# Mixer stage of a two-layer decoder step: prompt division in the transposing product, convolution norm with tokens on partitions, negated scores without scaling, and the pooling product ahead of output parts

## The reference

```python
def conv_mixer(a, prev, dw, dw_bias, ln_g, ln_b, pw):
    g = a[..., :CONV_W] * jax.nn.sigmoid(a[..., CONV_W:])
    buf = jnp.concatenate([prev.astype(g.dtype), g], axis=1)
    y = lax.conv_general_dilated(buf, ...) + dw_bias
    y = jax.nn.silu(layernorm(y, ln_g, ln_b)) @ pw      # 256 channels
    return y, buf[:, -(CONV_K - 1):]

def sparse_attend(q, ks, vs, valid):                    # 8 heads of 64, 2 key-value heads
    s = jnp.einsum('btngd,btknd->btngk', qg, ks.astype(jnp.float32)) * HEAD_DIM ** -0.5
    s = jnp.where(valid[:, :, None, None, :], s, -jnp.inf)
    p = jax.nn.softmax(s, axis=-1)
    o = jnp.einsum('btngk,btknd->btngd', p, vs.astype(jnp.float32))
    return o.reshape(B, T, ATTN_W).astype(q.dtype)
```

## Time and profile before

| | |
|---|---|
| median of 3 runs | 1144.7 us (1140.73 to 1146.01) |
| the profiled execution's own time | 1138.1 us |
| its span, first to last instruction | 1136.4 us |
| mean granted TensorE clock | 0.988 |
| TensorE busy | 1078.3 us, 95% of the span |
| VectorE busy | 740.0 us, 65% |
| ScalarE busy | 513.5 us, 45% |
| GpSimd busy | 190.0 us, 17% |
| stretch of the change, layer 1 | about 296 to 340 us from the span's start |
| the same, layer 2 | about 854 to 900 us |

### The profile page before, as it was taken

The page is one execution under the profiler, slowest core; times in us unless marked ns, Lnnn a source line. Parts: engine busy times, 40 slices in busy tenths (PEclk is TensorE's granted clock), DMA queues, the critical chain, the costliest instruction groups (busy, mean ns, idle before and its releaser), DMA issues.

```text
span 1136.4 us, 27658 instructions
## 1 busy us (share of the span) xinstructions
PE 1078.3 (95%) x9374; PEld 1024.2 (90%) x9374; DVE 740.0 (65%) x1211; ACT 513.5 (45%) x830; POOL 190.0 (17%) x241
## 2 busy tenths in 40 slices
PE   6999999999779999999999999999987899999996
PEld 5999999988459999999999999998873799999995
DVE  5667744688975766764476666448889466777544
ACT  5544443631454644443464444345216455444432
POOL 4211100411311311110042111004212022111001
PEclk9999999999899999999999999999998999999998
DMA  8464565443536455555435465563345445555541
GB/s 282 163 229 150 220 210 195 162 142 107 152 97 203 134 183 183 185 185 178 155 112 193 176 232 179 198 245 122 114 139 143 100 154 190 179 181 184 185 148 39
DMA packets 90464, 191.17 MB, mean 168 GB/s; under 512 B 12322, under 2 KB 48482, under 8 KB 90402
## 3 DMA queue, kind: packets, MB, share of 16 engines
q1 hardware_dynamic: 87426, 184.82, 48.7%
q0 software_dynamic: 2976, 5.53, 2.1%
HBM read 187.71 MB, written 2.59 MB: 167 GB/s over the span
## 4 chain that ended last, share of the span: by engine, by line
PE 85%; DVE 6%; ACT 4%; issue 2%; SPq 1%; DMA 1%; POOL 0%; DVEq 0%; POOLq 0%; ACTq 0%
PE PS L1111 24%; PE PS L1112 23%; PE PS L1113 23%; PE PS L1219 4%; PE PS L1147 2%; PE PS L1249 2%; DVE w_lo L601 1%; SPq L264 1%; PE PS L1158 1%; PE PS L1159 1%; PE PS L1162 1%; DVE rstd_post L630 1%; ACT w_hi L380 1%; PE PS L1225 1%; PE PS L1481 1%
## 5 line engine op out<-in xcount | busy, mean ns | idle before, releaser
L601 DVE TENSOR_TENSOR w_lo<-raw,w_hi 128x1024 fp32r<-128x1024 f32 x295 | 394.6, 1338 | 307.9 <-ACT w_hi L380 305.4
L380 ACT ACTIVATE w_hi<-raw 128x1024 fp32r<-128x1024 f32 x295 | 310.7, 1055 | 250.7 <-PE PS L1113 209.9
L1111 PE MATMUL PS<-x_hi,w_hi 128*128 128x264 f32 x1456 | 415.7, 286 | 0.7 <-DVE w_lo L601 0.6
L1112 PE MATMUL PS<-x_lo,w_hi 128*128 128x264 f32 x1456 | 412.6, 283 | 0.0
L1113 PE MATMUL PS<-x_hi,w_lo 128*128 128x264 f32 x1456 | 412.3, 283 | 0.0
L1111 PEld LDWEIGHTS PS<-x_hi,w_hi 128*128 128x128 f32 x1456 | 274.2, 188 | 2.3 <-DVE w_lo L601 1.6
L1112 PEld LDWEIGHTS PS<-x_lo,w_hi 128*128 128x128 f32 x1456 | 274.4, 188 | 0.1
L1113 PEld LDWEIGHTS PS<-x_hi,w_lo 128*128 128x128 f32 x1456 | 273.0, 188 | 0.0
L1111 PE MATMUL PS<-h_hi,w_hi 128*128 (+1 forms) x832 | 237.2, 285 | 3.7 <-DVE h_lo L1054 3.7
L1113 PE MATMUL PS<-h_hi,w_lo 128*128 (+1 forms) x832 | 236.9, 285 | 0.0
L1112 PE MATMUL PS<-h_lo,w_hi 128*128 (+1 forms) x832 | 236.2, 284 | 0.0
(11 more groups left out here) (255 smaller groups left out, 994.8 us busy)
## 6 DMA issues: line engine op xcount, KB each, us to landing
raw<-in_wts SPq DMA_DIRECT2D x312, 512.0 KB, 3.7
kv<-in_kT SPq DMA_DIRECT2D x128, 64.0 KB, 2.0
kx<-in_kxT SPq DMA_DIRECT2D x128, 32.0 KB, 2.1
vx<-in_vC POOLq DMA_DIRECT2D x48, 64.0 KB, 2.3
raw<-in_vC SPq DMA_DIRECT2D x32, 64.0 KB, 2.3
kv<-in_vC SPq DMA_DIRECT2D x32, 64.0 KB, 2.0
out_yT<-h SPq DMA_DIRECT2D x8, 132.0 KB, 1.8
vx<-in_vC SPq DMA_DIRECT2D x16, 64.0 KB, 1.8
```

Of the source, the lines that this page charges most:

```text
L380: act.activation(w_hi[:, u % SPLIT, :], raw[:, u % RAW, :], ACT.Copy) \
L601: tt(w_lo[:, u % SPLIT, :], raw[:, u % RAW, :], w_hi[:, u % SPLIT, :].bitcast(F32), AL.subtract) \
L1111: pe.matmul(out, w_hi[:, w, cols], hi, start=start, stop=False)
L1112: pe.matmul(out, w_hi[:, w, cols], lo, start=False, stop=False)
```

## The change

- Prompt division. The probabilities stay undivided. VectorE makes four diagonal matrices from the identity and the four inverted sums (`share`, 128 x 4 x 128), and TensorE multiplies each 128x128 block of the exponentials by its diagonal, which transposes and divides at once, in place of the transpose. `share` has one buffer for all pairs, so VectorE waits for the previous pair's products before it writes it.
- Negated scores. Masking computes mask minus scores, the maximum becomes a minimum, and the exponential has scale -1 with the minimum as its bias. The scale moves into the multiplier with which the queries are rotated (`turned`). The small multiplications of the extremum by the scale are gone, for the prompt's pairs and for the sample group.
- Convolution norm. The variance sums are made with tokens on the partitions: products of the squares with a column of ones give up to 128 tokens on partitions in each of three columns. ScalarE takes the root of these columns, VectorE inverts them (`inverted`, after `norm(1)`), and TensorE spreads them over all partitions by a product with the identity, behind pair 1's transposing products. `normalized` then multiplies from PSUM.
- The pooling product and the two transposes of the sample group's output stand ahead of `out_part(1, (0, 1))` and `out_part(2, (0, 1))`, the pooling product first.

```diff
@@ ScalarE
-                            ins = act.activation(t, t, ACT.Exp, scale=SCALE,
+                            ins = act.activation(t, t, ACT.Exp, scale=-1.0,
...
-                        act.activation(crs[:, :], PS[:, 6, 0:NT], ACT.Sqrt, scale=1.0 / 256,
-                                       bias=epsb[:, 0:1]).then_inc(sem["c_rms"], 1)
+                        act.activation(crt[:, 0:2], PS[:, 6, 0:2], ACT.Sqrt, scale=1.0 / 256, bias=epsb[:, 0:1])
+                        act.activation(crt[0:NB, 2:3], PS[0:NB, 6, 2:3], ACT.Sqrt, scale=1.0 / 256,
+                                       bias=epsb[0:NB, 0:1]).then_inc(sem["c_rms"], 1)
...
-                act.activation(psm[:, :], psm[:, :], ACT.Exp, scale=SCALE,
-                               bias=smx[:, 1:2], accum_out=smx[:, 2:3]).then_inc(sem["p_sexp"], 1)
+                act.activation(psm[:, :], psm[:, :], ACT.Exp, scale=-1.0,
+                               bias=smx[:, 0:1], accum_out=smx[:, 2:3]).then_inc(sem["p_sexp"], 1)
@@ VectorE
-                turned(9, aq[:, 0, :])
+                turned(9, aq[:, 0, :], SCALE)
...
-                    linked(stt(s, bias[:, :].unsqueeze(1).to_broadcast([128, 2, 384]), -BIG, PS[:, 2:4, 0:384],
-                               AL.mult, AL.add))
-                    dve.tensor_reduce(spm[:, j % 2, 0:4:2], s[:, :, 0:256], AX.X, AL.max)
-                    k = step(L, dve.tensor_reduce(spm[:, j % 2, 1:4:2], s[:, :, 256:384], AX.X, AL.max))
-                    after(L, k)
-                    ts(spm[:, j % 2, :], spm[:, j % 2, :], -SCALE, None, AL.mult).then_inc(sem["s_masked"], 1)
+                    linked(stt(s, bias[:, :].unsqueeze(1).to_broadcast([128, 2, 384]), BIG, PS[:, 2:4, 0:384],
+                               AL.mult, AL.subtract))
+                    dve.tensor_reduce(spm[:, j % 2, 0:4:2], s[:, :, 0:256], AX.X, AL.min)
+                    dve.tensor_reduce(spm[:, j % 2, 1:4:2], s[:, :, 256:384], AX.X, AL.min) \
+                        .then_inc(sem["s_masked"], 1)
...
-                    for b, (lo, hi) in enumerate(((0, 256), (256, 384))):
-                        t = sp_[:, j % 2, :, lo:hi]
-                        ins = tt(t, t, sps[:, j % 2, b:4:2].unsqueeze(2).to_broadcast([128, 2, hi - lo]), AL.mult)
-                    ins.then_inc(sem["p_norm"], 1)
+                    if j:
+
+                        dve.wait_ge(sem["p_t"], at_layer(L, "p_t", 2 * j))
+                    tt(share[:, :, :], ident.unsqueeze(1).to_broadcast([128, 4, 128]),
+                       sps[:, j % 2, :].unsqueeze(2).to_broadcast([128, 4, 128]), AL.mult).then_inc(sem["p_norm"], 1)
...
+                def inverted():
+
+                    dve.wait_ge(sem["c_rms"], at_layer(L, "c_rms", 1))
+                    dve.reciprocal(crt[:, 0:2], crt[:, 0:2])
+                    dve.reciprocal(crt[0:NB, 2:3], crt[0:NB, 2:3]).then_inc(sem["c_inv"], 1)
+
                 def normalized():
 
-                    dve.wait_ge(sem["c_rms"], at_layer(L, "c_rms", 1))
-                    linked(dve.reciprocal(crs[:, :], crs[:, :]))
+                    dve.wait_ge(sem["c_wide"], at_layer(L, "c_wide", 1))
                     for c in range(2):
-                        ins = tt(cacc[:, c, :], cacc[:, c, :], crs[:, :], AL.mult)
+                        ins = tt(cacc[:, c, :], cacc[:, c, :], PS[:, 6, 0:NT], AL.mult)
...
                 norm(1)
+                inverted()
                 masked(2)
...
-                linked(dve.reduce_max(smx[:, 0:1], psm[:, :], AX.X))
-                ts(smx[:, 1:2], smx[:, 0:1], -SCALE, None, AL.mult).then_inc(sem["s_smax"], 1)
+                dve.tensor_reduce(smx[:, 0:1], psm[:, :], AX.X, AL.min).then_inc(sem["s_smax"], 1)
@@ TensorE
-                            ins = pe.transpose(PS[:, (7, 0)[a], 128 * n:128 * n + 128], p[:, c:c + 128], ident)
+                            ins = pe.matmul(PS[:, (7, 0)[a], 128 * n:128 * n + 128], p[:, c:c + 128],
+                                            share[:, 2 * a + c // 256, :], start=True, stop=True)
...
                         pe.wait_ge(sem["c_sq"], at_layer(L, "c_sq", 1))
-                        channel_sum(csq, "c_var")
+                        for b, n in enumerate((128, 128, NB)):
+                            for c in range(2):
+                                ins = pe.matmul(PS[0:n, 6, b:b + 1], csq[:, c, 128 * b:128 * b + n], ones[:, 0:1],
+                                                start=(c == 0), stop=(c == 1))
+                        ins.then_inc(sem["c_var"], 1)
+                    if j == 1:
+                        pe.wait_ge(sem["c_inv"], at_layer(L, "c_inv", 1))
+                        for b, n in enumerate((128, 128, NB)):
+                            ins = pe.matmul(PS[:, 6, 128 * b:128 * b + n], crt[0:n, b:b + 1].to_broadcast([n, 128]),
+                                            ident[0:n, 0:n], start=True, stop=True)
+                        ins.then_inc(sem["c_wide"], 1)
...
                 values(1)
-                out_part(1, (0, 1))
-                out_part(2, (0, 1))
+                pe.wait_ge(sem["pool_y"], at_layer(L, "pool_y", 1))
+                for c in range(2):
+                    ins = pe.matmul(PS[:, 4 + c, 0:NT], raw[:, w, col(4 + c)], pw[:, c, :], start=True, stop=True)
+                ins.then_inc(sem["unit_done"], 1)
                 pe.wait_ge(sem["o_sc"], at_layer(L, "o_sc", 1))
                 for c in range(2):
                     ins = pe.transpose(PS[:, 7, 128 * c:128 * c + 128], osb[:, c, :], ident)
                 ins.then_inc(sem["o_st"], 1)
-                pe.wait_ge(sem["pool_y"], at_layer(L, "pool_y", 1))
-                for c in range(2):
-                    ins = pe.matmul(PS[:, 4 + c, 0:NT], raw[:, w, col(4 + c)], pw[:, c, :], start=True, stop=True)
-                ins.then_inc(sem["unit_done"], 1)
+                out_part(1, (0, 1))
+                out_part(2, (0, 1))
```

More of the change, by code:

```diff
@@ L88 @@
     o_shi=1, o_slo=1, dg=1,
-    tanh=2, glu=2, stack=1, diag=2, conv=1, c_part=4, c_fold=1, conv_p=1, c_sum=1, c_cent=1, c_sq=1, c_var=1, c_rms=1, c_norm=1, c_silu=1,
+    tanh=2, glu=2, stack=1, diag=2, conv=1, c_part=4, c_fold=1, conv_p=1, c_sum=1, c_cent=1, c_sq=1, c_var=1, c_rms=1, c_inv=1, c_wide=1, c_norm=1, c_silu=1,
     conv_r=1, c_out=1, c_ohi=1, c_olo=1,
@@ L168, in build @@
         X = place("X", [128, NS], F32, s1)
-        crs = place("crs", [128, NT], F32, s1)
         assert s1[0] <= s1_end
         ties = place("ties", [128, NS], F32, [s2[0]])
+        share = place("share", [128, 4, 128], F32, [s2[0] + 4128])
         relu = place("relu", [128, 4, 256], F32, s2)
@@ L214, in build @@
         spread = place("spread", [128, 128], F32)
+        crt = place("crt", [128, 4], F32)
         assert s_kx[0] <= kx_end and s_gs[0] <= gs_end and s_sq[0] <= s_gs0
@@ L721, in rope, with turned @@
                     tt(x, x, tmp, AL.add).then_inc(sem["rope"], 1)
-                def turned(m, x):
+                def turned(m, x, scale=1.0):
                     turns[0] += 1
                     src = PS[:, m % 2, 0:NT]
-                    chunk(m, (x, src, (1.0, turn[:, 0, :])), (rtmp[:, turns[0] % 2, :], src, (1.0, turn[:, 1, :])))
+                    chunk(m, (x, src, (scale, turn[:, 0, :])), (rtmp[:, turns[0] % 2, :], src, (scale, turn[:, 1, :])))
                 def rope_end(x, bank):
@@ L875, in mixer @@
                 p0 = count(0)
-                turned(10, aq[:, 1, :])
+                turned(10, aq[:, 1, :], SCALE)
                 rope_end(aq[:, 0, :], 2)
@@ L879, in mixer @@
                 p1 = count(1)
-                turned(11, aq[:, 2, :])
+                turned(11, aq[:, 2, :], SCALE)
                 rope_end(aq[:, 1, :], 2)
@@ L883, in mixer @@
                 p2 = count(2)
-                turned(12, aq[:, 3, :])
+                turned(12, aq[:, 3, :], SCALE)
                 rope_end(aq[:, 2, :], 2)
@@ L1025, in mixer @@
                 dve.wait_ge(sem["s_s"], at_layer(L, "s_s", 1))
-                stt(psm[:, 0:PAST], Z[:, 0:PAST], BIG, PS[:, 4:6, :].rearrange("p a b -> p (a b)"),
-                    AL.mult, AL.add)
-                linked(stt(psm[:, PAST:], Z[:, PAST:], BIG, PS[:, 2, 0:1], AL.mult, AL.add))
-                linked(dve.reduce_max(smx[:, 0:1], psm[:, :], AX.X))
-                ts(smx[:, 1:2], smx[:, 0:1], -SCALE, None, AL.mult).then_inc(sem["s_smax"], 1)
+                stt(psm[:, 0:PAST], Z[:, 0:PAST], -BIG, PS[:, 4:6, :].rearrange("p a b -> p (a b)"),
+                    AL.mult, AL.subtract)
+                linked(stt(psm[:, PAST:], Z[:, PAST:], -BIG, PS[:, 2, 0:1], AL.mult, AL.subtract))
+                dve.tensor_reduce(smx[:, 0:1], psm[:, :], AX.X, AL.min).then_inc(sem["s_smax"], 1)
                 heads_out(3)
```

## The result

The changed kernel takes 1134.1 us (median of 8 runs, 1131.8 to 1137.4) against 1143.6 for the kernel before in the same comparison; the ratio is 0.992, 95% interval 0.990 to 0.9945. A second comparison gave 0.993 (0.991 to 0.9955). By the two ratios the gain is 7.5 to 9 us.

The account below looks back on a forecast made before the run. TensorE, busy 95% of the span, was taken as the bound, held at the second key product by SyncE's key transfers. Layer 1 (-1.7 + 0.1) and layer 2 (-1.7 + 0.35) gave about -3.0 us: 1144.7 to 1141.7, range 1136.5 to 1146.

Parts of the forecast that it names:

- The wall of the key transfers: Second key product, both layers: it waits for the last of SyncE's 32 key transfers, so VectorE's savings ahead count nothing.
- the wall isn't one: Second key product: VectorE's savings count and two waits of 3.8 us go as well, 1137.9 us; chance 0.08.
- over 2 us of idle time: Sign ahead of the second key product: more TensorE idle time in both layers, still ended by the transfer.
- The shrinking wait: Sign at the second key product (L1363): if TensorE's wait there shrinks, the prediction is wrong.
- The pooling move: Pooling product ahead of output parts 1 and 2: TensorE goes on at about 338.0 instead of 339.71, 1.7 us gained a layer.
- The last pair's products: Doubled passes behind the second key product: 0.35 us lost a layer, net 0.1 in layer 1 and 0.35 in layer 2.
- VectorE's wait for the square root: Convolution norm, before pair 2's scores: VectorE waits 0 to 1 us for ScalarE, hidden; over 2 us would refute.
- Nothing in the diff is ahead of the first key product: Second key product's starts, 319.11 in layer 1 and 877.16 in layer 2, stay, however fast VectorE becomes.
- rival (b): Layer 2's second key product: the clock stays up because doubled products give TensorE more work; 1.72 us less, 1140.0; chance 0.12.
- (a): Layer 1: the granted clock falls ahead of the second key product; price 1.72 us or a little less, 1143.4; chance 0.25.
- (c): Both layers: clock at 0.50 from the second key product to the exponential; +3.3 us, 1148.0; chance 0.06.
- The base: Profiled execution of 1138.1 us, from which the sum was made; the 6.6 us up to the median 1144.7 was carried over.

Follow-up runs that it names:

- long fills: Changed kernel plus idle float32 products of ones in three TensorE waits (3, 3 and 3 of 512 columns): ratio 0.996, mean 1137.1 us.
- padding: 19 tiny float32 products a layer ahead of TensorE's first wait for probabilities: added to the kernel before, ratio 0.998; added to the changed kernel, 0.997.
- short fills: Changed kernel plus idle products of ones in three TensorE waits (7, 6 and 7 of 128 columns): ratio 0.993, mean 1134.3 us.
- run 34: Not a run number: the mean run of the unchanged kernel before had 34 us at half clock; its mean time is 1141.7 us over 130 runs.
- identity products: Kernel before with its 24 transposes a layer made as float32 products with the identity, VectorE's division left as it was: ratio 1.000, mean 1141.9 us.

## Why the prediction was wrong, step by step

- **The wall of the key transfers: right.** 18.4 to 19.7 us from first issue to product in 32 readings, whatever the kernel, and 8.4 us less work on VectorE gave nothing. Only layer 2 of the changed kernel's first profile and the long fills show no wait in front of the product: there TensorE arrived with it. The rival "the wall isn't one" falls. But the sign given for it, over 2 us of idle time ahead of the product in both layers, was wrong: the two profiles of the change have 2.58 and 0, and 1.32 and 0.92, where those of before have 1.81 and 1.98, and 0.58 and 2.31. The shrinking wait that was to refute the prediction came, and the start relative to the first issue didn't move. In layer 2 TensorE's own work ahead of it, with twice the passes, ended later: 19.0 and 18.7 us after the first issue, before 16.8 and 16.6.
- **The pooling move: right**, mechanism and, as far as the runs can tell, size. Product at 335.01, other work to 337.8, restart at 338.05 with 0.21 us of wait, where 338.0 and 0.1 to 0.2 were forecast; 1.66 us from this in layer 1. The weights' queue started at 336.24 instead of 337.92. Given all the rest, the move is worth 3.7 us in the means (1137.9 to 1134.2); alone it measured 1.9, with an interval that takes in 3.4 and nothing.
- **The last pair's products: not refuted, too small to see.** From the key product to the exponential it is 7.56 us in layer 1 of the change; the two profiles of before have 7.28 and 7.83, which differ by more than the 0.1 forecast. In layer 2 the key product's clock differs, so the 0.35 can't be read.
- **VectorE's wait for the square root: right.** 0.78 us in layer 1 and 0.31 in layer 2, forecast at 0 to 1, and hidden.
- **The step that failed: "Nothing in the diff is ahead of the first key product, so 319.11 and 877.16 stand."** True of the work and of layer 1. But 877.16 became 873.45, 2.3 us of it in the third section. In layer 2 everything that layer 1 adds to TensorE's stream is ahead of the taps, and in the taps, with a record every 22 ns, TensorE stalls for "issue". In the five profiles with 9450 matmul records the stall in layer 2's taps is 1.8 to 3.0 us, in the eight with fewer 6.0 to 7.2, in the three with more 4.5 to 6.1 (of TensorE's matmuls alone: 0.4 to 1.0, 2.35 to 2.99 and 1.7 to 2.3). In layer 1, where nothing is added ahead of them, it is 5.1 to 7.5 in all, and 5.2 and 7.3 in the same kernel before. The sum had no term for this. By the padding it is worth 2 to 3 us of the missing 4.5. That the instructions ahead of the taps decide, and not those behind them, is argued from layer 1; no run pads only one side. The row that could have warned was in the list of waits that I began with, the second largest entry of all: L1249 waiting 5.0 us for "issue". I left it out because no edited line was in it.
- **The clock: rival (b) by its sign, not by its price.** The changed kernel has 10 us less at half clock, and its key product in layer 2 took 1.92 us in both profiles, not 3.64 as in both of before. In layer 1 it took 1.92 in all four, so rivals (a) and (c) didn't come. That the pairs of profiles agree speaks against a mere draw in layer 2, though two are few. But some 8 to 12 us less in the kernels with doubled TensorE work gave nothing clear, and 11.6 us fewer through short fills gave nothing in the mean beside a third section 3.5 us longer. It is a share of the gain that I can't separate from the rest; what is left for it, after 3.4 for the pooling move and 2 to 3 for the stall, is 1 to 2 us. Another estimate is higher: among the 130 runs of the kernel before, the time rises by 0.36 us for each us at half clock (correlation 0.91), which for 10.5 us less would be 3.8. Between these the share stays open, the more so as some falls of the clock stand right behind the stalls.
- **The base: a good execution.** The profile summed over had 27 us at half clock, the mean run 34. I carried the difference to the median over as a constant; half of 7 us is 3.5, more than the whole forecast, and a change that alters the clock alters it. The two profiles of before lie 3.2 us under their kernel's mean, those of the change 0.6 under theirs. So the gain of 7.5 us in the means splits, by the averages of the two pairs of profiles, into three parts of about 2.5: 2.6 us in the two sections from keys to weights, where the sum had its 3.0; 2.4 in the third section, where it had nothing; and 2.6 by which this distance shrank, where it also had nothing.
- **The size: the sum was right for its own stretch, the range wasn't wide enough for the rest.** The direction was no luck. The two missing terms are together larger than everything that was summed.

## What to carry to other kernels

Read the waits for "issue" as a row of its own before saying that a stretch doesn't change: an edit that adds or removes instructions on an engine can move a later stretch in which that engine stalls for "issue", and 38 matmul records a layer of no use were worth as much here as a real edit. Test it with padding before crediting an edit. And where a queue issues transfers one after another from a fixed event, work taken off the engines ahead of the last landing is worth nothing, as 8.4 us of VectorE's were here.

## What the runs showed of the hardware

- The stalls of a dense burst of small matmuls went with the number of records added to TensorE's stream: 2.99 us of idle time with none added, 0.76 with 38 a layer, 2.32 with 76 a layer. What TensorE waits for there no row shows (the profile has only "issue"), and neither is the period of the pattern known.
- Behind such a stall the granted clock fell in some profiles: to 0.57 from 846 to 850 us in the kernel with all but the division, 0.66 and 0.63 from 850 to 854 with the division alone and the identity products.
- Float32 transposes made twice lowered the time at half clock from 36.2 us in the runs beside them to 24.5, as real products did (27.2). So float32 transposes count for TensorE's clock here.
- The scatter of the kernel before (3.3 us, one standard deviation over 130 runs) goes with the time at half clock (correlation 0.91): the clock's falls are most of what differs between runs of that kernel. Across kernels it is not so plain: 1.6 us for the full change (23.9 at half clock) and 0.6 for the short fills (12.3), but 1.3 without the division (31.8) and 1.2 for the long fills (12.1).
- A float32 pass of 512 columns took 0.47 us in the long fills (six in 2.84), one of 128 columns 0.13 (twelve in 1.60).
